# A two-block network on one Trainium2 core: weight splits moved to GpSimd, and parts of five engines' orders exchanged

## The reference

```python
# first block, two layers
for i in range(2):
    h = rmsnorm(x, norm1_g[i])
    x = x + hybrid_mixer(h, w_in[i], ...) @ w_out[i]
    h = rmsnorm(x, norm2_g[i])
    a, u = split(h @ w_up[i])                 # 2 x 2816
    x = x + (silu(conv3(a) + conv_b) * u) @ w_down[i]
x = rmsnorm(x, final_g)
# second block, one layer
u = rms_norm(x, norm_mix_pre)
a_x, a_gate, p_x, c_q, c_f, c_i, c_g, s_b, s_c, s_x, gate_logits = split(u @ w_in_2)
ys = [rg_lru(a_x, a_gate), pool(p_x), hgrn2(c_q, c_f, c_i, c_g), short_conv(s_b, s_c, s_x)]
merged = sum(sigmoid(gate_logits[k]) * (ys[k] @ w_branch[k]) for k in range(4))
x = x + rms_norm(merged @ w_out_2, norm_mix_post)
x = x + rms_norm(square(relu(rms_norm(x, norm_mlp_pre) @ w_up_2)) @ w_down_2, norm_mlp_post)
```

## Time and profile before

| | us |
|---|---|
| median of 3 runs | 1082.15 (1080.23 to 1083.16) |
| the profiled execution's own time | 1080.23 |
| its span, first to last instruction | 1078.9 |
| TensorE busy | 1047.6 (97%) |
| VectorE busy | 777.9 (72%) |
| ScalarE busy | 539.7 (50%) |
| GpSimd busy | 244.2 (23%) |
| mean granted TensorE clock | 0.993 |

### The profile page before, as it was taken

One profiled execution on the slowest core, in us unless ns is written; L12 is line 12 of the kernel. 1 busy time (PEld: TensorE's weight loads), 2 busy tenths in 40 slices (PEclk: granted clock), 3 DMA queues, 4 the chain that ended last, 5 costly groups with the idle time before them and its releaser, 6 DMA issues.

```text
span 1078.9 us, 15736 instructions
## 1 busy us (share of the span) xinstructions
PE 1047.6 (97%) x6184; PEld 888.5 (82%) x6186; DVE 777.9 (72%) x1256; ACT 539.7 (50%) x797; POOL 244.2 (23%) x335
## 2 busy tenths in 40 slices
PE   8999899999999999899999999999999899999997
PEld 6777688888888767688888888998999867888886
DVE  6987568787777987568787778976655447666665
ACT  5454566555456454566455456654334435433432
POOL 1362610000000362600000003147967620000000
PEclk9989999999999999999999999999999999999999
DMA  9341345555555341355555554444445454555441
GB/s 364 128 174 60 117 157 191 200 167 204 196 179 189 119 168 39 118 202 194 196 195 183 195 177 149 156 142 149 140 145 173 170 198 156 215 193 197 161 151 39
DMA packets 26713, 179.22 MB, mean 166 GB/s; under 512 B 2960, under 2 KB 2960, under 8 KB 6160
## 3 DMA queue, kind: packets, MB, share of 16 engines
q1 hardware_dynamic: 26640, 178.22, 47.5%
HBM read 177.16 MB, written 1.05 MB: 165 GB/s over the span
## 4 chain that ended last, share of the span: by engine, by line
PE 88%; DVE 6%; ACT 4%; POOL 2%; issue 1%; DVEq 0%; ACTq 0%; POOLq 0%
PE pb L598 18%; PE pb L599 9%; PE pb L624 6%; PE pb L626 6%; PE pb L625 6%; PE pb L536 5%; PE pb L537 5%; PE pb L539 5%; PE pb L561 4%; PE pb L562 3%; PE pb L563 3%; PE pb L603 3%; POOL wlo L2388 2%; PE pb L602 1%; PE pb L850 1%
## 5 line engine op out<-in xcount | busy, mean ns | idle before, releaser
L1573 DVE TENSOR_TENSOR wlo<-raw,whi 128x2048 fp32r<-128x2048 f32 x124 | 284.6, 2297 | 114.2 <-ACT whi L1153 114.2
L1153 ACT ACTIVATE whi<-raw 128x2048 fp32r<-128x2048 f32 (+1 forms) x165 | 305.0, 1852 | 57.7 <-PE pb L626 22.0
L598 PE MATMUL pb<-hb,whi 128*128 128x512 f32 x840 | 302.1, 398 | 0.9 <-DVE hb L1595 0.9
L2388 POOL TENSOR_TENSOR wlo<-raw,whi 128x256 fp32r<-128x256 f32 x284 | 215.3, 793 | 332.3 <-ACT whi L1153 332.0
L599 PE MATMUL pb<-hb,wlo 128*128 128x256 f32 x840 | 236.2, 281 | 0.0
L598 PEld LDWEIGHTS pb<-hb,whi 128*128 128x128 f32 x840 | 158.3, 188 | 35.0 <-issue 1.1
L599 PEld LDWEIGHTS pb<-hb,wlo 128*128 128x128 f32 x840 | 159.2, 190 | 5.1
L624 PE MATMUL pb<-whi,gh 128*128 128x512 f32 x288 | 114.1, 396 | 0.0
L626 PE MATMUL pb<-whi,gl 128*128 128x512 f32 x288 | 114.1, 396 | 0.0
L625 PE MATMUL pb<-wlo,gh 128*128 128x512 f32 x288 | 114.0, 396 | 0.0
L561 PE MATMUL pb<-hb,whi 128*128 128x256 f32 x376 | 108.1, 287 | 2.3 <-DVE PQ L2310 1.4
(11 more groups left out here) (365 smaller groups left out, 1596.5 us busy)
## 6 DMA issues: line engine op xcount, KB each, us to landing
raw<-wst SPq DMA_DIRECT2D x160, 1024.0 KB, 4.9
raw<-wst SPq DMA_DIRECT2D x8, 512.0 KB, 3.6
gb<-gains SPq DMA_DIRECT2D x3, 512.0 KB, 5.9
X<-x SPq DMA_DIRECT2D x4, 256.0 KB, 6.6
out<-X SPq DMA_DIRECT2D x4, 256.0 KB, 2.0
PQ<-prm SPq DMA_DIRECT2D x1, 909.0 KB, 4.5
prmt<-prm SPq DMA_DIRECT2D x1, 547.0 KB, 5.9
raw<-wst SPq DMA_DIRECT2D x2, 256.0 KB, 7.1
```

The source lines that it names most:

```text
L598: e.matmul(both, wh[:, k, s], hb2[:, k, :, :].rearrange("p i q -> p (i q)"), start=k == 0, stop=False)
L1153: e.activation(whi[:, split_slot(m), 0:w], raw[:, m % RAW, 0:w], ACT.Copy).then_inc(*hi(m))
L1573: e.tensor_tensor(wlo[:, split_slot(m), 0:w], raw[:, m % RAW, 0:w], whi[:, split_slot(m), 0:w].bitcast(F32), ALU.subtract).then_inc(*lo_v(m))
L2388: g = e.tensor_tensor(wlo[:, split_slot(m), s], raw[:, m % RAW, s], whi[:, split_slot(m), s].bitcast(F32), ALU.subtract)
```

## The change

It changes six things. (1) `on_pool`: in the second block all gate tiles and all four `out` tiles have their low part on GpSimd; before, VectorE had the gate tiles with odd qq of the last two branches, and two of the `out` tiles. That is six tiles. (2) In the attention TensorE does scores(4) ahead of part(3, 1, 0), scores(5) ahead of part(3, 1, 1), and last_values behind scores(6); ScalarE does weights(4) and the split behind it ahead of turned(3), and weights(5) ahead of the two evictions of projection 3; GpSimd does the low part of the tile that is two behind in(3, 1), out(0, 0), ahead of its rope for `qc`. (3) The pool branch's product, eviction and keep_y(1) go from the first gate to the third (TensorE) and fourth (ScalarE, VectorE). (4) ScalarE issues `ahead(2, "branch", ...)` behind the step of `deep`, no longer in front of it. (5) VectorE clears PT itself, after its running sums; before, GpSimd did. (6) VectorE does the two pairs of operations on g1 ahead of the split `ahead(2, "in", 0, 0)`.

```diff
--- before.py
+++ after.py
@@ -327,9 +327,7 @@
             _, l, name, j, _, _ = plan[m]
             if l < 2:
                 return name == "out" or name == "in" and j in (2, 3, 5)
-            if name == "gate":
-                return BRANCHES.index(j) < 2 or plan[m][4] % 2 == 0
-            return name == "branch" or name == "out" and plan[m][4] == 0 or name == "tok" and plan[m][4] == 1
+            return name in ("gate", "branch", "out") or name == "tok" and plan[m][4] == 1
 
         def lo_of(m):
             return lo_g if on_pool(m) else lo_v
@@ -932,17 +930,17 @@
                 q.wait_ge(*ce_turned[l])
                 values(0, 4, 5)
                 turned(2)
+                scores(4)
                 part(3, 1, 0)
                 values(1)
                 values(2)
                 turned(3)
-                scores(4)
+                scores(5)
                 part(3, 1, 1)
                 values(3)
-                scores(5)
-                last_values()
                 turned(4)
                 scores(6)
+                last_values()
                 evicted(3)
                 q.wait_ge(*roped_g[l, "qc"])
                 transposed(11, 12)
@@ -1106,7 +1104,7 @@
                     for half in range(2):
                         for qq in gates_of(n == 0, half):
                             gate(n, qq)
-                            if n == 0 and qq == 0:
+                            if n == 0 and qq == 2:
                                 pool_mixed()
                             if deep:
                                 step = deep.pop(0)
@@ -1344,12 +1342,12 @@
                 weights(3)
                 transposed(9)
                 turned(2)
-                turned(3)
                 weights(4)
                 ahead(l, "in", 3, 1)
+                turned(3)
+                weights(5)
                 project(3, 0, 6)
                 project(3, 1, 7)
-                weights(5)
                 turned(4)
                 weights(6)
                 ahead(l, "in", 5, 0)
@@ -1502,7 +1500,7 @@
                                 q.wait_ge(*(b_used[0, qq] if n == 2 else b_used[1, qq, "sum"]))
                             e.activation(GT[:, n % 2, 2 * qq:2 * qq + 2, :], halves(gate_bank(n, qq)), ACT.Tanh,
                                          scale=0.5).then_inc(*gated(n, qq))
-                            if n == 0 and qq == 0:
+                            if n == 0 and qq == 3:
                                 q.wait_ge(*mm_small["pool"])
                                 q.wait_ge(*dve["pool diff"])
                                 for f in range(2):
@@ -1511,12 +1509,9 @@
                                 a.then_inc(*act("pool out"))
                                 q.wait_ge(*q.prev)
                                 keep_y(1, s4)
-                            if qq == gates_of(n == 0, half)[-1]:
-                                ahead(2, "branch", k, half)
                             if going:
                                 going = next(deep, "end") != "end"
-                        if not gates_of(n == 0, half):
-                            ahead(2, "branch", k, half)
+                        ahead(2, "branch", k, half)
                         if n == 1 and half:
                             q.wait_ge(*dve["lru out"])
                             keep_y(2, th[:, :, :])
@@ -2109,6 +2104,7 @@
                         v = e.tensor_tensor_scan(bs[:, f, :], par2("reset"), lf[:, f, :], 0.0, ALU.mult, ALU.add)
                     v.then_inc(*dve("sums"))
                     yield
+                    e.memset(PT[:, :, :], 0.0).then_inc(*dve("SC zero"))
 
                     def queries(i, src, pick, dec):
                         for hf in range(2):
@@ -2203,7 +2199,6 @@
                 next(deep)
                 ahead(2, "in", 3, 0)
                 next(deep)
-                ahead(2, "in", 0, 0)
                 for t in range(2):
                     q.wait_ge(*act["tokens", t])
                     e.scalar_tensor_tensor(g1[:, t, :], g1[:, t, :], 1.0, PB[4 + t][:, 256:512], ALU.add,
@@ -2213,6 +2208,7 @@
                 for t in range(2):
                     v = e.scalar_tensor_tensor(g1[:, t, :], g1[:, t, :], z[:, t:t + 1], par2("hn"), ALU.mult, ALU.mult)
                 v.then_inc(*dve())
+                ahead(2, "in", 0, 0)
                 lcw = par2("lcw")
                 q.wait_ge(*act["xc"])
                 for f in range(2):
@@ -2411,7 +2407,7 @@
                     q.wait_ge(*proj(l, 2, t))
                 q.wait_ge(s_prm, 16)
                 rope(e, q, rt_g, pool, roped_g(l, "qb"), C_QB + 64, 8, 64, 8, "cosh", "sinh")
-                m = ahead_to(m, l, "in", 3, 0)
+                m = ahead_to(m, l, "in", 3, 1)
                 for t in range(2):
                     q.wait_ge(*proj(l, 3, t))
                 rope(e, q, rt_g, pool, roped_g(l, "qc"), C_QC + 256, 8, 64, 8, "cosh", "sinh")
@@ -2429,7 +2425,7 @@
                 e.tensor_tensor(zf[:, 6 + t:7 + t], z[:, 4 + t:5 + t], half[:, 0:1], ALU.pow).then_inc(*powed("final", t))
             m = ahead_to(m, 2, "tok", 0, 1)
             q.wait_ge(*dve["log f"])
-            for zz in (Z[0], Z[1], rl[:, :, :], PT[:, :, :]):
+            for zz in (Z[0], Z[1], rl[:, :, :]):
                 g = e.memset(zz, 0.0)
             g.then_inc(*zero_g("scan"))
             m = ahead_to(m, 2, "gate", BRANCHES[2], 1)
```

## The result

| | before | changed |
|---|---|---|
| median, same chip, 4 runs each | 1081.19 us (1079.59 to 1083.16) | 1097.79 us (1095.81 to 1099.18) |
| profiled execution, its span | 1080.23, 1078.9 us | 1097.97, 1096.6 us |
| mean granted TensorE clock | 0.993 | 0.985 |

The ratio is 1.0151, with a 95% interval of 1.0126 to 1.0177: the change makes the kernel 16.6 us slower. The forecast was 1099 us.

What follows compares the result with a forecast made beforehand. TensorE bounds the kernel, busy 1047.6 of 1078.9 us, so only its waits and clock matter. 1080.2 us plus 8.2 (attention), 5.2 (second block) and 5.1 (clock falls) gave 1098.7, said as 1099 us; range 1090.5 to 1106.

Steps and rivals of the forecast that it cites:

- stands for the mask, two layers: Attention: TensorE reaches scores(4) before VectorE's selection mask is ready and stands 5.9 us per layer.
- wait at L818 comes back: Attention: turned(5)'s wait for ScalarE's eviction goes whole, as last_values moves behind scores(6); 1.8 us back per layer.
- (a): Start of second block: VectorE's PT clearing and g1 operations ahead of the split delay a low part; +1.0 us.
- (b): First gate: pool out and keep_y(1) no longer stand before VectorE's level(1), whose product waited; -1.9 us.
- (c): Fourth gate: pool out, keep_y, level and exponential now precede the split for gate tile g10; +4.7 us.
- (d): Gate tile g01: its split waits for the exponential and its low part moves to GpSimd; +2.0 us.
- (e): Gate tile g03: GpSimd first does a power of 3.63 us, so its low part comes late; +2.7 us.
- (f): From g03 to the last out tile: GpSimd sets the pace, 76 pieces at 0.77 us; -3.3 us.
- Rival 1: The clock doesn't fall, since activity around the stands holds it; 1093.6 us, 18 in 100.
- rival 2: Second block: GpSimd keeps up without VectorE's long splits, pieces at 0.70 us; 1093.2 us, 14 in 100.
- Rival 3: Second block: GpSimd's pieces stay at 0.89 us; 1111 us, 8 in 100.
- rival 4: VectorE, freed of six splits, feeds the second block early enough that TensorE never waits there; 1077.1 us, 2 in 100.

Runs made afterwards that it cites:

- last_move: Kernel before with one edit: last_values behind turned(4) and scores(6) on TensorE, both layers; 1081.0 us, ratio 0.9996.
- att_late: Kernel before with scores(4) behind values(2), scores(5) behind part(3,1,1), last_values behind scores(6), ScalarE's weights(4) ahead of turned(3); 1081.78 us, ratio 0.9999.
- att_undone: Changed kernel with the attention's part undone, all the rest left; 1085.05 us, ratio 1.0036.
- stall_filled: Changed kernel with six throw-away products of 512 float32 columns in front of scores(4); 1091.61 us, ratio 1.0091.
- att_only: Kernel before with only the attention's part of the change; 1094.37 us, ratio 1.0111.
- g10_first: Changed kernel, but ScalarE's split for the tile two behind a half's last gate again in front of the deep step; 1090.8 us, ratio 1.0092.
- s4_later: Changed kernel with scores(4) moved back one place, behind part(3,1,0); 1088.51 us, ratio 1.0066.
- mask_free: Changed kernel, but pair 4, the first DSA pair, takes the constant causal mask, not VectorE's selection; 1082.63 us, ratio 1.0006.
- pool_only: Kernel before with `on_pool` alone changed, six more tiles on GpSimd in the second block; 1079.95 us, ratio 0.9995.
- best2: best1 with att_late's attention order besides, and the pool branch's eviction and keep_y(1) at the third gate; 1077.89 us, ratio 0.9962.
- best1: att_undone with the edits of last_move and g10_first; 1078.91 us, ratio 0.9979.

## Why the prediction was right, by its own steps

| step | predicted | measured |
|---|---|---|
| stands for the mask, two layers | +11.8 | +10.6 |
| wait at L818 comes back | -3.6 | -3.5 |
| wait at L882, not foreseen | 0 | +1.4 |
| wait at L896 (now L894) gone, not foreseen | 0 | -0.7 |
| clock in the attention | +3.4 | +6.1 |
| (a) start of the second block | +1.0 | +0.3 |
| (b) and (c) up to g10 | +2.8 | +2.2 |
| clock behind g10 | +1.7 | +1.5 |
| (d) g01 | +2.0 | +2.3 |
| (e) g03 | +2.7 | +1.0 |
| (f) from g03 to the MLP | -3.3 | -3.6 |
| sum | 18.5 | 17.6 |

The measured column is read from waits and from the differences of starts given above; the clock in the attention is what is left of its 13.9 us after the four rows on waits. The mechanism and the two largest terms were right. That the sum came within 1 us is luck in part: the clock in the attention and the wait at L882 brought 4.1 us more than forecast, and the stands, L896, (a), (c) and (e) together nearly 5 us less.

**The attention.** The stand was read rightly from one time stamp, the mask's, and one start, part(3,1,0)'s. What came back has the right size and the wrong reason. The prediction gave it to "last_values moved behind scores(6)"; last_move shows 1.1 of 3.5 us for that. The rest comes from the other edits of this stage: scores(5) ahead of part(3,1,1), weights(5) ahead of the evictions on ScalarE, or GpSimd's order, which the prediction took at nothing. Which of them it needs stays open; att_late shows that scores(5) a little earlier isn't enough. The step looked at TensorE's 24 products in front of turned(5) and not at what ScalarE's split itself waits for. L882 (L884 before) isn't a cost of the change: att_undone, with the old attention, has the 1.4 us too, and every other trace but that of the kernel before has 0.7 to 1.8 us there in one layer or both. The kernel before has none where its clock was down just ahead (391.6 us); so this term and the 1.7 us of that fall belong to the one execution that was traced.

**The clock.** The prediction took 1.7 us per fall; the two in the stands ran 4.44 and 4.14 us of TensorE's work at half the clock, 2.2 and 2.1 us, and the one at 409.4 us 3.2 us; less the 1.7 us of the fall at 391.6 us that the kernel before had and this one hasn't, 5.8 us. stall_filled's trace gives 5.8 us for the same, and what is left in the table is 6.1. The prediction's term was too small since it took the length of a fall, 3.4 us, from one row; the same trace has one of 6.8 us at 67 us. Rival 1, that the clock stays up, is refuted by the stretches at 0.50; with the clock up in the attention, in stall_filled, the kernel takes 1091.6 us, near the 1093.6 us that it was priced at (the fall behind g10 is still in it). That the long stands bring the falls is well borne out: att_only and g10_first, the other two kernels with the stands of 5.0 to 6.0 us, have both falls too, and of the others only s4_later has one there, behind a stand of 3.2 us. The Trainium skill, TensorE: Matmul & The Clock Gate, Part 1, that an idle TensorE drops to the lower clock: by that rule, the trace agrees for the long stands, while the two stands of 3.2 us in s4_later went both ways. Why the clock fell at 409.4 us stays open; mask_free, pool_only and best2, which have no stand, have a fall of 6.8 us from 402 to 404 us on, too.

**The second block.** (b) the wait at L1013 shrank from 1.92 to 0.76 us, and a new one of 1.51 us came at the products of the deep step behind the fourth gate, whose bank the late pool eviction holds (in best2, with the eviction a gate earlier, it is gone); the prediction named the eviction's move and not its bank. (c) "TensorE then stands there for about 6 us" was wrong in the size: it stood 3.13 us, since the new waits ahead of g10 had taken part of the delay; the sum of (b) and (c) was off by 0.6 us. (d) had the right size, but the low part's change of engine, which it named beside the late split, has no share in it: with GpSimd's low part and the early split g10_first has under 0.3 us of wait. (e) was too high because GpSimd's power took 1.65 us, not the 3.63 us of the earlier trace rows, and its pieces 0.74 us, which the timeline of GpSimd of the changed kernel shows:

```profile
833.10 1.65 POOL L2433 TENSOR_TENSOR sm<-sm 128x8 f32<-128x8 f32 x1 [1.83 <-DVE sm L2182]
834.71 14.87 POOL L2384 TENSOR_TENSOR wlo<-raw,whi 128x256 fp32r<-128x256 f32 x20
...
865.12 15.53 POOL L2384 TENSOR_TENSOR wlo<-raw,whi 128x256 fp32r<-128x256 f32 x20 [0.23 <-ACT whi L1151]
```

Twenty pieces take 14.9 and 15.5 us, 0.74 and 0.78 us each, against rival 2's 0.70 and the forecast's 0.77. The 84 pieces from g03 to the last `out` tile run from 834.7 to 899.2 us with pauses of 0.7, 0.2 and 0.2 us, 0.77 us a piece; (f) is right, and by its own mechanism. Rival 3 (0.89 us) and rival 4 are refuted. What rival 4 hoped for is real, but small: best1 and best2 are what the second block's part of the change can give, 2 to 3 us. One side sum of the prediction is too small: with 4.5 us for eight pieces, (c), (d) and (e) would be 4.7 us lower by its rows, as it says, but (f) would also fall to its bound of -7.1, and the sum would be some 8.5 us smaller, not 5 (an estimate).

## What to carry to other kernels

Before a step is moved ahead in the order of the engine that sets the pace, look up when its last input is ready; each microsecond by which the new place is sooner is a stand, and the clock that falls in it can add half as much again. A wait that a move seems to free belongs to a chain: follow it back over all engines to the first step that could be earlier, or the move gives a part of what was counted (here a third). Two edits that are free one by one (a late pool branch, a late split) can cost 7 us together, when one delays what the other waits for; undo them one at a time from the changed side, too.

## What the runs showed of the hardware

**Throw-away work can pay.** Filling two stands of 5.6 and 5.0 us with six float32 products each gave back 6.2 us by the medians, most of it by the clock. The trace also lacks the fall at 409.4 us in front of the second stand; whether the filling took it away isn't shown, since falls near there come and go from trace to trace.

**VectorE and GpSimd in each other's way.** The same three VectorE operations with one SBUF tensor and a scalar take 0.68 us in the changed kernel, while GpSimd is idle, and 1.94 us in mask_free, while GpSimd makes a low part (99.49 to 105.06 us). The timelines of VectorE, first the changed kernel, then mask_free, and that of GpSimd in mask_free:

```profile
108.54 0.68 DVE L1973 TENSOR_SCALAR XN<-XN,sm 128x128 f32<-128x128 f32 x3
```

```profile
102.51 1.94 DVE L1973 TENSOR_SCALAR XN<-XN,sm 128x128 f32<-128x128 f32 x3
```

```profile
99.49 5.57 POOL L2384 TENSOR_TENSOR wlo<-raw,whi 128x256 fp32r<-128x256 f32 x8 [16.48 <-ACT whi L1151]
```

GpSimd's eight pieces keep their 0.70 us each there; VectorE's short operations pay. The Trainium skill, SBUF — State Buffer, section "SBUF: two separate sides", has the two engines hold a shared port pair one at a time for a whole instruction, and the section "Who interferes with whom" counts some VectorE operations with one input, tensor_scalar among them, as ones that can need it. By that rule, the trace agrees as to VectorE's times. So splits moved to GpSimd can slow more than VectorE's products of two SBUF operands, which alone the prediction had in mind.
